# Hybrid pooling/state-space block with experts: residual sum through ScalarE, a turned router product, a sorted choice, and three modulation blocks in another place

## What is computed

```python
mod_x = silu(c) @ w_mod + b_mod                 # 1 x 6144: sh1, sc1, g1, sh2, sc2, g2
hx = modulate(rmsnorm(x, g_mix), sh1, sc1)
ux = hx @ w_in                                  # half to pooling, half to the state-space scan
x = x + g1 * (concat([pool_x, ssm_x]) @ w_out)
hx2 = modulate(rmsnorm(x, g_ffn), sh2, sc2)
s = sigmoid(hx2 @ w_router)                     # 32 experts in 4 groups
sel = s + b_router                              # best group by the sum of its two best, then two experts in it
y = sum over the two chosen experts of gate * (silu(h @ w_gate[e]) * (h @ w_up[e])) @ w_down[e]
x = x + g2 * y
return rmsnorm(x, g_final)
```

## Time and profile before

| | |
|---|---|
| median of 3 runs | 642.79 us (641.74 to 643.32) |
| the profiled execution | 646.29 us, its span 644.2 us |
| busy in it: PE, DVE, ACT, POOL | 590.5, 196.5, 134.9, 49.2 us |
| moved by DMA | 246.93 MB, mean 383 GB/s |

### The profile page before, as it was taken

How to read it: one execution, slowest core, us unless ns; L and a number is a source line. 1 busy time by engine, 2 the same in 40 slices (tenths; PEclk the granted TensorE clock), 3 DMA queues, 4 the chain that set the end, 5 groups by cost and what they waited for, 6 DMA issues and landing times.

```text
span 644.2 us, 9383 instructions
## 1 busy us (share of the span) xinstructions
PE 590.5 (92%) x3790; PEld 247.9 (38%) x3790; DVE 196.5 (31%) x428; ACT 134.9 (21%) x238; POOL 49.2 (8%) x101
## 2 busy tenths in 40 slices
PE   1999999899999798999999899969988996999996
PEld 0454565464553242334334233423332342334331
DVE  7998499987630010002002001000100020001003
ACT  7761243041122111012111110202020111012112
POOL 3795000010000000000000000000000000000001
PEclk9999999899689999999999899979998998999999
DMA  8997785999879999999999999999999999999992
GB/s 311 422 398 268 273 300 185 371 397 410 365 272 420 421 365 423 421 421 386 425 422 421 423 422 422 423 420 422 423 422 422 423 418 423 422 421 419 419 402 88
DMA packets 43497, 246.93 MB, mean 383 GB/s; under 512 B 4664, under 2 KB 7368, under 8 KB 17616
## 3 DMA queue, kind: packets, MB, share of 16 engines
q1 hardware_dynamic: 41960, 243.93, 93.0%
q10 hardware_dynamic: 1160, 1.59, 0.7%
q0 software_dynamic: 352, 1.07, 0.6%
HBM read 244.46 MB, written 2.11 MB: 383 GB/s over the span
## 4 chain that ended last, share of the span: by engine, by line
PE 61%; DMA 16%; ACT 1%; DVE 0%; issue 0%; SPq 0%; POOL 0%; POOLq 0%; DVEq 0%
PE ps L927 26%; PE ps L978 17%; DMA wts<-in_w_up 16%; PE ps L894 4%; PE ps L900 3%; PE ps L857 2%; PE ps L943 1%; PE ps L763 1%; ACT ra L1211 1%; PE ps L819 1%; PE ps L830 1%; PE ps L779 1%; PE ps L808 1%; PE ps L807 1%; PE ps L959 0%; PE ps L849 0%
## 5 line engine op out<-in xcount | busy, mean ns | idle before, releaser
L927 PE MATMUL ps<-wts,ra 128*64 128x512 f32 x504 | 234.3, 618 | 23.3 <-DMA wts<-in_w_up 23.3
L928 PE MATMUL ps<-wts,ra 128*64 128x512 f32 x504 | 234.3, 618 | 0.0
L927 PEld LDWEIGHTS ps<-wts,ra 128*64 128x64 f32 x504 | 68.4, 141 | 168.5 <-issue 135.3
L978 PE MATMUL ps<-wts,ra 128*32 128x512 f32 x512 | 111.6, 593 | 0.7 <-DVE ra L1271 0.7
L978 PE MATMUL ps<-rc,ra 128*32 128x512 f32 x512 | 111.6, 593 | 0.0
L1271 DVE TENSOR_TENSOR ra<-ra,ps 128x256 f32<-128x256 f32 x32 | 13.5, 421 | 259.5 <-ACT ra L1217 259.5
L1211 ACT COPY ra<-ps 128x512 f32<-128x512 f32 x32 | 33.5, 1046 | 217.4 <-PE ps L928 217.4
L928 PEld LDWEIGHTS ps<-wts,ra 128*64 128x64 f32 x504 | 68.4, 141 | 0.0
L978 PEld LDWEIGHTS ps<-wts,ra 128*32 128x32 f32 x512 | 29.1, 110 | 74.1 <-issue 73.1
L1271 DVE TENSOR_TENSOR cb<-ps,ra 128x512 f32<-128x512 f32 x32 | 22.1, 691 | 102.7 <-PE ps L978 102.7
L1206 ACT COPY ra<-ps 128x512 f32<-128x512 f32 x32 | 18.7, 585 | 144.3 <-PE ps L894 144.3
(11 more groups left out here) (238 smaller groups left out, 537.3 us busy)
## 6 DMA issues: line engine op xcount, KB each, us to landing
wts<-in_w_up SPq DMA_DIRECT2D x63, 1024.0 KB, 16.7
wts<-in_w_gate SPq DMA_DIRECT2D x63, 1024.0 KB, 15.0
rc<-in_w_down SPq DMA_DIRECT2D x28, 1024.0 KB, 21.2
wts<-in_w_down SPq DMA_DIRECT2D x28, 1024.0 KB, 17.4
wts<-in_w_mod SPq DMA_DIRECT2D x16, 1024.0 KB, 13.1
r<-in_w_mod SPq DMA_DIRECT2D x6, 1024.0 KB, 5.9
wts<-in_w_out SPq DMA_DIRECT2D x2, 2048.0 KB, 14.3
wts<-in_w_down SPq DMA_DIRECT2D x6, 512.0 KB, 16.4
```

Of the source, the lines that this page charges most:

```text
L927: pe.matmul(ps[0:64, 4 + b, :], st, gate_k, start=(k == 0), stop=(k == KD - 1))
L928: mm = pe.matmul(ps[64:128, 4 + b, :], st, up_k, start=(k == 0), stop=(k == KD - 1))
L978: mm = pe.matmul(ps[32 * j:32 * j + 32, BANKS[n], :], hid[:, j, f, SLOTS * t:SLOTS * t + SLOTS], Wd[j][:, f, 512 * h:512 * h + 512], start ...
```

## The change

It has five parts.

1. `start_output` goes from TensorE. ScalarE copies x2 into the four banks of PSUM after it has copied the gate, and `outs_started` now counts two of these copies.
2. The router's product is turned round: 32 columns of router weights are the stationary side, 128 token columns move, and the eight blocks of channels go to four groups of 32 partitions, two added in each. DVE copies the result (`take_logits`), and a product with four stacked identities adds the four groups and brings tokens back to partitions. The last block of the mix is split into two of 256 columns (the second in bank 7), and residual, `scaled` and transposes follow in finer pieces. The copy out of PSUM for channels 512 to 1023 of the second token tile is in two pieces.
3. The choice uses MAX8 (the eight largest, sorted) instead of `first_best` for the two experts: the second largest is the threshold, and ties are cut by a rank.
4. The gate's bias is added by GpSimd (`mod_bias(1)`) and no longer by two TensorE products, and the four `rows` pieces are five, in another order around the counts.
5. The second third of `w_mod`: blocks 0 to 2 stood between `u_ssm(1)` and `u_ssm(2)` and now stand behind `state_inputs(0)`; block 5 and 6 stand behind `turn_lags(7)` and in `u_pool`. Blocks 3 and 4 are loaded early into the place of `wo_ssm`, whose load now comes after them, and the loads of blocks 5 to 7 come behind the second `u8_load`. One product of `mix_pool(2)` stands ahead of the wait for the scan.

The diff, cut to its core (GpSimd's and the small changes of TensorE's waits are left out):

```diff
-        wm2 = [wm[1], wm[2], wm[0], cb[:, 2048:4096]]
+        wm1 = [wm[2], wm[0], wm[1], wts[:, 20480:22528], wts[:, 22528:24576], wm[2], wm[0], wm[1]]
+        wm2 = [wm[2], wm[0], wm[1], cb[:, 2048:4096]]
+        MOD1_IN = (("wmod_in2", 16), ("wmod_in0", 16), ("wmod_in1", 16), ("wblock_in4", 32), ("wblock_in5", 32),
+                   ("wmod_in2", 32), ("wmod_in0", 32), ("wmod_in1", 32))
...
+            def mod_chunk(k):
+                sp.wait_ge(S("mod_used"), (3, 8, 2, 4, 5, 9, 10, 11)[k])
+                sp.dma_start(wm1[k], w_mod[0, k * P:(k + 1) * P, 2048:4096]).then_inc(S(MOD1_IN[k][0]), 16)
...
-            for k in range(3):
-                mod_chunk(1, k)
-            sp.wait_ge(S("mod_used"), 5)
-            sp.dma_start(wo_ssm, w_out[0].rearrange("(k p) n -> p k n", p=P)[:, 4:8, :]).then_inc(S("wo_ssm_in"), 16)
+            for k in range(5):
+                mod_chunk(k)
...
                 sp.wait_ge(S(f"u_out{h}"), 16)
                 u8_load(sp, h, range(L // 2 if h else L))
-                for k in range(3 + 3 * h, min(6 + 3 * h, KD)):
-                    mod_chunk(1, k)
...
+            for k in range(5, KD):
+                mod_chunk(k)
+            sp.wait_ge(S("mod_used"), 13)
+            sp.dma_start(wo_ssm, w_out_v[:, 4:8, :]).then_inc(S("wo_ssm_in"), 16)
             sp.wait_ge(S("mod_used"), 14)
             last_third(0, 0)
...
             u_ssm(1)
-            pe.wait_ge(S("ks_copy"), 1)
-            for k in range(3):
-                mod_chunk(1, k, 6)
             u_ssm(2)
             u_ssm(3)
             pe.wait_ge(S("st_copy"), 16)
             state_inputs(0)
+            pe.wait_ge(S("ks_copy"), 1)
+            for k in range(3):
+                mod_chunk(1, k, 6)
             turn_lags(0)
             turn_lags(1)
-            for k in range(3, 6):
+            for k in range(3, 5):
                 mod_chunk(1, k, 6)
             turn_lags(2)
             turn_lags(3)
+            state_inputs(1)
             pe.wait_ge(S("win_pool_in"), 16)
-            u_pool(0, range(4))
-            state_inputs(1)
+            u_pool(0, range(2))
             turn_lags(4)
             turn_lags(5)
-            u_pool(0, range(4, KD))
+            u_pool(0, range(2, 6))
             turn_lags(6)
             turn_lags(7)
+            mod_chunk(1, 5, 6)
+            u_pool(0, range(6, KD))
+            mod_chunk(1, 6, 6)
             u_pool(1, range(KD))
-            mod_chunk(1, 6, 6)
...
+            mix_pool(2, (0,))
...
                 if m < 3:
-                    mix_pool(2, (m,))
+                    mix_pool(2, (m + 1,))
             mm.then_inc(S("y_mm"), 1)
-            mix_pool(2, (3,))
             mix_pool(3, (0,))
...
-            mix_pool(3, (1,))
+            mix_pool(3, (1, 2, 3), cols=slice(0, 256))
...
-                pe.wait_ge(S("mod2_used"), 2 * KD)
+                pe.wait_ge(S("mod2_sum"), 4)
                 for h in range(2):
                     j = 2 + h
-                    pe.matmul(ps[:, 6 + h, :], ones[32 * j:32 * j + 1, :], modrow[32 * j:32 * j + 1, 2, :], start=True, stop=False)
-                    mm = pe.matmul(ps[:, 6 + h, :], ones, acc[:, 512 * j:512 * j + 512], start=False, stop=True)
+                    mm = pe.matmul(ps[:, 6 + h, :], ones, acc[:, 512 * j:512 * j + 512], start=True, stop=True)
...
-            mix_pool(3, (2, 3)).then_inc(S("mix_pool"), 1)
-            def start_output(n):
...
+            pe.wait_ge(S("a2b_ready"), 1)
+            mix_pool(3, range(4), 7, slice(256, 512)).then_inc(S("mix_pool"), 1)
+            def turn_rows(t, ks, bank):
+                for k in ks:
+                    mm = pe.transpose(ps[:, bank, 128 * (k % 4):128 * (k % 4) + 128], hn[t][:, P * k:P * k + P], ident)
                 mm.then_inc(S("xa_t"), 1)
...
+            def logits(t, ks):
+                for k in ks:
+                    q = k % 4
+                    mm = pe.matmul(ps[32 * q:32 * q + 32, 7 - t, 0:P], wrt[:, k, :], xaT[:, t, k, :],
+                                   start=(k < 4), stop=(k >= 4), skip_group_check=True)
+                return mm
...
+            pe.wait_ge(S("wo_ssm_in"), 16)
+            mix_ssm(0, 0).then_inc(S("mix_mm"), 1)
+            pe.wait_ge(S("shift_prod"), 1)
+            pe.matmul(ps[:, 6, 0:NE], ones, cpart, start=True, stop=True).then_inc(S("shift_mm"), 1)
+            mix_ssm(1, 1).then_inc(S("mix_mm"), 1)
+            mix_ssm(2, 2).then_inc(S("mix_mm"), 1)
+            mix_ssm(3, 3, slice(0, 256)).then_inc(S("mix_mm"), 1)
+            for half in range(2):
+                pe.wait_ge(S("xa_ready"), half + 1)
+                turn_rows(0, range(4 * half, 4 * half + 4), 4 + half)
+            mix_ssm(3, 7, slice(256, 512)).then_inc(S("mix_mm"), 1)
             pe.wait_ge(S("shift_copy"), 1)
-            turn_rows(1, 0)
+            pe.wait_ge(S("xa_ready"), 3)
+            turn_rows(1, range(0, 4), 6)
+            pe.wait_ge(S("xat_act"), 2)
+            pe.wait_ge(S("xa_ready"), 4)
+            turn_rows(1, range(4, 6), 4)
+            pe.wait_ge(S("xa_ready"), 5)
+            turn_rows(1, range(6, 8), 5)
             pe.wait_ge(S("wr_in"), 16)
-            logits(0)
-            turn_rows(1, 1)
-            logits(1)
-            start_output(0)
-            start_output(1)
+            logits(0, range(KD)).then_inc(S("logit_mm"), 1)
+            pe.wait_ge(S("xat_act"), 3)
+            logits(1, range(4))
+            pe.wait_ge(S("turned"), 2)
+            logits(1, range(4, KD)).then_inc(S("logit_mm"), 1)
+            for t in range(NT):
+                pe.wait_ge(S("turned"), t + 3)
+                pe.matmul(ps[:, 4 + t, 0:NE], lgp[:, t, :], stack4, start=True, stop=True,
+                          skip_group_check=True).then_inc(S("logit_mm"), 1)
             gate_product().then_inc(S("gate_mm"), 1)
             pe.wait_ge(S("score"), 1)
...
             act.copy(g2b, ps[:, 6:8, :].rearrange("p a n -> p (a n)")).then_inc(S("g2_ready"), 1)
+            for t in range(NT):
+                act.copy(ps[:, 2 * t:2 * t + 2, :].rearrange("p a n -> p (a n)"), x2[:, t, :]).then_inc(S("outs_started"), 1)
...
+            def take_logits(t):
+                dve.wait_ge(S("logit_mm"), t + 1)
+                dve.tensor_copy(lgp[:, t, :], ps[:, 7 - t, 0:P]).then_inc(S("turned"), 1)
...
+            def take_turned(ks, n):
+                dve.wait_ge(S("xa_t"), n)
+                at = slice(128 * (ks.start - 4), 128 * (ks.stop - 4))
+                dve.tensor_copy(xaT[:, 1, ks, :], ps[:, ks.start // 2 + 2, at].rearrange("p (k q) -> p k q", q=128)).then_inc(S("turned"), 1)
...
             scaled(1, 0, 512)
-            rows(0, 0)
             dve.wait_ge(S("mix_mm"), 4)
-            residual(1, 512, 512).then_inc(S("x2_ready"), 1)
+            link(residual(1, 512, 256))
+            scaled(1, 512, 256)
+            dve.wait_ge(S("xa_ready"), 2)
+            rows(0, slice(0, 4))
+            dve.wait_ge(S("mix_mm"), 5)
+            residual(1, 768, 256).then_inc(S("x2_ready"), 1)
             dve.wait_ge(S("x2_ready"), 2)
-            scaled(1, 512, 512)
-            dve.wait_ge(S("xa_t"), 4)
-            dve.tensor_copy(xaT[:, 1, 4:8, :], ps[:, 7, :].rearrange("p (k q) -> p k q", k=4)).then_inc(S("xat_dve"), 1)
-            dve.wait_ge(S("xa_ready"), 3)
+            scaled(1, 768, 256)
+            take_turned(slice(4, 6), 4)
+            take_turned(slice(6, 8), 5)
+            take_logits(0)
+            take_logits(1)
             logit(0)
             logit(1)
-            rows(1, 0)
-            link(dve.tensor_scalar(rank, iota[:, 0:NE], -1.0, float(NE), ALU.mult, ALU.add))
+            dve.wait_ge(S("xa_ready"), 5)
+            rows(1, slice(0, 2))
...
             link(tt(sel4, sel4, gmx, ALU.min))
-            first_best(one1, sel, rank, NE)
-            link(dve.scalar_tensor_tensor(sel.rearrange("p t e -> p (t e)"), one1.rearrange("p t e -> p (t e)"), -HUGE * 4,
-                                          sel.rearrange("p t e -> p (t e)"), ALU.mult, ALU.add))
-            first_best(one2, sel, rank, NE)
-            tt(msk, one1, one2, ALU.add).then_inc(S("chosen"), 1)
+            for t in range(NT):
+                ins = dve.max(two[:, t], sel[:, t])
+            link(ins)
+            for t in range(NT):
+                dve.scalar_tensor_tensor(one1[:, t], sel[:, t], two[:, t, 1:2], rank, ALU.is_ge, ALU.mult)
+            link(tt(one2, sel, two[:, :, 1:2].broadcast_to([P, NT, NE]), ALU.is_gt))
+            link(dve.scalar_tensor_tensor(one1.rearrange("p t e -> p (t e)"), one2.rearrange("p t e -> p (t e)"), 2.0 * NE,
+                                          one1.rearrange("p t e -> p (t e)"), ALU.mult, ALU.add))
+            for t in range(NT):
+                ins = dve.max(two[:, t], one1[:, t])
+            link(ins)
+            tt(msk, one1, two[:, :, 1:2].broadcast_to([P, NT, NE]), ALU.is_ge).then_inc(S("chosen"), 1)
             dve.wait_ge(S("chosen"), 1)
...
```

(11 more changed lines are left out.)

99 lines of the change are left out of this document (39 added, 60 removed).

## The result

The changed kernel takes 638.21 us (median of 20 executions, 636.76 to 641.46), the kernel before, in executions between them, 642.17 us (20, 640.22 to 646.25). The ratio is 0.9929 (0.9914 to 0.9944): 4.6 us faster by the ratio, 4.0 by the two medians, where 10.0 were forecast. The direction was right; the size was less than half, and the time lies above the forecast's 632.8 (630.5 to 634.8) and just outside the wider range of 630 to 638. The profiled execution of the changed kernel took 638.94 us (span 637.0), 0.7 above its median; the one of before took 646.29, 4.1 above its own. That difference turns out to be the heart of the case.

The account below looks back on a forecast made before the run. One long stream of loads at 422 GB/s plus its idle time bounds the kernel. Path terms summed to 12.1 us, less 1.7 for the clock; the stream allowed 10.2. Forecast: 642.8 - 10.0 = 632.8 us (630.5 to 634.8).

Parts of the forecast that it names:

- what the stream can give back: DMA idle time ahead of the experts that the change could remove: at most 7.1 + 1.0 + 2.1 = 10.2 us.
- Step (d): Router: identity products and gate's bias off TensorE, so counts follow the choice at once, 4.6 us, plus 1.7 around the gathers.
- The 1.7 behind the slots: Around the gathers: identity products of 1.8 and 0.86 us go, a `rows` piece comes between; gain 1.7 us.
- Step (a): Ahead of the scan: three w_mod blocks moved behind the first half's states; gain 2.5 us (1.2 to 2.7).
- (b): Residual and router logits: finer residual pieces and turned router product; gain 2.3 us (bounds 1.0 and 2.6).
- (c): DVE's choice of experts: MAX8 in place of two rounds of reduce and compare; gain 1.0 us.
- The clock, 1.7: Gathers and expert 0: TensorE idles some 3.5 us for the choice, then runs slow; 1.7 us lost (0 to 3.4).
- rival 2: Clock alone: gathers and whole first half of expert 0 slow, gain 8.3 us, 634.5; chance 0.1, inside another rival's 0.25.
- The 2.1 us at 124 to 136: Stream loss at 349 GB/s there, to be won because the four gate blocks are asked for 3.7 us sooner.
- The hole at the down projection: 4 us from 226 at 195 GB/s, 2.2 us lost; claimed to move with the stream and stay.
- Rival 3: Hole of 174 reappears at 226, TensorE reaching the down projection no sooner: 640 to 643; chance 0.05.
- Rival 1: Path ahead of the experts falls short, gaining 5 to 8 us, stream idles for the rest: 634.8 to 638; chance 0.25.

Follow-up runs that it names:

- second profile: The kernel before, unchanged, profiled and timed once more: 642.53 us, ratio 1.002; the profiled execution took 641.47 us.
- outs_in_front: Changed kernel with the gate's bias and identity products back on TensorE, in the order of the kernel before: 638.3 us, ratio 0.9932.
- block6_back: Changed kernel with the seventh w_mod block behind the second pooling product again: 636.75 us, ratio 0.9922 to the kernel before.
- blocks_only: Kernel before with only the w_mod blocks moved (part 5 of the change), old router kept: 640.04 us, ratio 0.9973.
- fill_wait: Changed kernel with three products of no use in TensorE's 3.45 us wait for the choice: 638.01 us, ratio 0.9937 to the kernel before.
- outs_in_wait: Changed kernel with identity products back on TensorE, three in its wait for the choice, one behind the counts: 637.69 us, ratio 0.9929.

## Why the prediction was wrong in size

**The step that failed: what the stream can give back.** The prediction said "7.1 + 1.0 + 2.1 = 10.2 us", and of the 3.5 us between the profiled execution and the median, "I take the difference over". Those 3.5 us were not beside the hole, they were in it. The profiled execution was one in which TensorE is granted 1.2 GHz (0.50) for 17 us of router work; its hole of 7.1 us is 2.0 in the second profile, whose time is that of the usual execution. The sum should have started from 2.0. The table of times gave the sign: 646.29 lies outside 641.74 to 643.32, and the clock of 0.50 stood in the very rows that carried the sum.

**Step (d), 4.6 + 1.7, the largest term.** It was right for the execution in the trace (counts directly behind the choice, as forecast), and nothing for the second: there TensorE is done 1.1 us ahead of the choice, and `outs_in_front` has the same time without it. "The gate product is now half (4.0 of 8.0 us at that clock)" was priced at a clock that the change does not meet. The 1.7 behind the slots came in and was lost to the clock, as the sum had it: from the counts to the first product the kernel before took 5.9 us in the first profile (177.76 to 183.61), the changed one takes 5.8. Against the second profile of before (4.8 us) it is a loss of 1.0.

**Step (a), 2.5.** The scan ended at 118.0, as forecast (118.3). The third piece started at 121.43, not 120.3: the prediction did not see that block 6 had covered ScalarE's copy of the second pooling product. It cost 1.1 us, and `block6_back` puts the piece at 120.31. The pieces are faster, as forecast (1.16 us each), but inside the last one TensorE now stands 1.37 us without a wait that the profile shows, where it stood 0.47 before; why, stays open. At the GLU product the gain is 1.3 (137.17 to 135.86) of 2.5. The blocks alone (`blocks_only`) give 2.3 there, without the half-wide quarters that the sum counted at 0.45.

**Steps (b) and (c), 2.3 and 1.0.** The second logits came 3.0 us sooner and the sum behind the sigmoid 3.7 (164.19 against 167.85), less 1.3 for (a): 2.4. Against the second profile of before (167.12) it is 1.5: 0.8 us of the step were half clock in the trace. The choice took 1.2 us less in both. So (c) held; (b) held in size for the execution in the trace, and at like clock it lies inside its bounds (1.0 to 2.6).

**The clock, 1.7.** In size right: gathers 3.75 us in place of 2.02, and `fill_wait` shows that the idle time brings it. The Trainium skill, TensorE: Matmul & The Clock Gate, section "The HAM clock gate", was cited for rival 2 as saying just this. Here the traces agree with it for the 3.45 us wait: 0.50 to 0.54 from 168 to 174 us, 1.00 again from 176. They do not agree for the busy stretch: it ran at 1.00 in one execution and at 0.50 in another, and that was the larger effect, with the other sign: the usual execution of the kernel *before* was the fast-clocked one.

**The 2.1 us at 124 to 136** were won there (408) and lost ahead (306 at 108 to 124), because blocks 5 to 7, and with them `last_third` and GLU's weights, are asked for later (GLU's weights at 110.00 against 108.79); the stream leads by 0.7 us at 174.

**The hole at the down projection** "moves with the stream and stays": it moved and lost 3.6 us, but it did so in the second profile of before too (3.9), so it is no loss of the change. Rival 3's mark, "a hole near 216 of over 3 us", was met by it, and rival 3 is still wrong: the hole at 174 is gone and TensorE reaches the down projection sooner.

**Rival 1** had almost the time (634.8 to 638), but not for its reason: it wanted a path too short and a stream that idles for the rest. The path gained 9.2 us against the first profile and 3.2 against the second, and either way the hole that the rival wanted at 168 to 190 us is closed (421). It came near by luck.

**The gain as it was.** At like clock (second profile of before, 641.47, against 638.94) it is 2.5 us. The stretches give 3.0: 2.0 of hole, 0.7 ahead of it, 0.3 at the down projection. The path is 3.2 us shorter (177.60 to 174.43), of which 1.2 find no hole. Measured are 4.0 by the medians and 4.6 by the ratio. The 1.5 to 2.1 us between are not explained: the profile of before lies 0.7 below its median and that of the changed kernel 0.7 above, which says how large the scatter of a single execution is, and not where the time goes. The small group of before carries little of it, since one of its 20 executions here (646.25) is as long as that group, which weighs 0.2 us in a mean.

That kernels with the new router have no such group is borne out by their executions (one of 91 below 0.971, and not a long one); that this is because TensorE is idle and not busy behind the router is argued, not shown: `outs_in_front` is busy there and shows no long execution either, in only six. What decides the clock at 164 us in the kernel before stays open, since the work ahead of it is the same in both traces.

## What to carry to other kernels

Where the profiled execution lies outside the timed ones, take its difference as a part of the sum that is still to be found: look first whether a stretch that carries an argument has a granted clock that another execution may not have, and price each step at both clocks. Here the largest term moved work off an engine that was slow in 14 of 74 executions: it was worth 4.6 us in the trace and nothing that the medians show. In a kernel bound by a stream of loads, add up its holes, and ask of each what releases the next load: here a finer release (a quarter in place of a half) left 0.4 us of a hole of which the shorter paths left 2. And compare kernels by ratios taken side by side before calling a gain of 1 us shown.

## What the runs showed of the hardware

- Same program, same work within 0.2 us up to 163.6 us: one execution goes on at 1.00, the other at 0.50 (from 164 to 181 us, TensorE busy all the time). In `blocks_only` it was 0.63, 0.80 and 0.77 in the stretches from 164 to 176 us, TensorE busy all the time again. 14 of 74 executions of the kernel before are some 4.4 us longer with a mean clock lower by 0.01.
- After 3.45 us idle the granted clock was 0.50 to 0.54 from 168 to 174 us in the changed kernel; after 0.79 to 0.88 us (`fill_wait`, `outs_in_wait`) it stayed 1.00. Ahead of expert 3 it fell in four profiles after 2.1 to 2.5 us idle, and stayed in eight after 1.7 to 2.3.
- Loads keep to 421 or 422 GB/s from 320 to 600 us in every trace; quarters of 512 KB moved 415 over the stretch where they were used.
